# Moving the end of each projection half two dense parts further on in a stick-breaking attention stage

## The reference, cut to what matters

```python
x = x + 0.5 * swiglu(rmsnorm(x, ffn1_norm))
h = rmsnorm(x, mix_norm)
q_sb, k_sb, v_sb, q_d, k_d, v_d, q_x, gates = split(h @ w_in)
...
o_sb = stick_breaking(q_sb, k_sb, v_sb)          # 6 heads of 64
#   z = q k^T / 8; log_keep = log_sigmoid(-z) below the diagonal
#   a = exp(log_sigmoid(z) + sum of log_keep over later keys); o = a v
o_dil = dilated(q_d, k_d, v_d); o_x = memory_attention(q_x, mem)
x = x + merge(gates, o_sb, o_dil, o_x) @ w_out
x = x + 0.5 * swiglu(rmsnorm(x, ffn2_norm))
```

## Time and profile before

| | us |
|---|---|
| median of three runs (2323.61 to 2325.2) | 2324.48 |
| the profiled execution's own time | 2322.87 |
| its span, first to last instruction | 2321.1 |
| PE busy / DVE busy / ACT busy / POOL busy | 2293.4 / 1146.5 / 619.7 / 137.6 |
| PE busy in 0 to 60 us | 52.23 of 60 |
| PE busy in 785 to 1030 us (the stick-breaking stage and its rims) | 233.65 of 245 |
| PE busy in 1030 to 2321 us | 1284.11 of 1291 |

### The profile page before, as it was taken

How to read it: one execution, slowest core, us unless ns; L and a number is a source line. 1 busy time by engine, 2 the same in 40 slices (tenths; PEclk the granted TensorE clock), 3 DMA queues, 4 the chain that set the end, 5 groups by cost and what they waited for, 6 DMA issues and landing times.

```text
span 2321.1 us, 25822 instructions
## 1 busy us (share of the span) xinstructions
PE 2293.4 (99%) x10616; PEld 1855.9 (80%) x10616; DVE 1146.5 (49%) x1119; ACT 619.7 (27%) x800; POOL 137.6 (6%) x108
## 2 busy tenths in 40 slices
PE   8999999999999999999999999999999999999999
PEld 7888888888887766777778888888888888888887
DVE  8444443434445777778636333435434434444434
ACT  6211111111112567856443111224111111111111
POOL 3000000000001311222000000011000000000000
PEclk9999999999999999999999999999999999999999
DMA  5211111111112200011122111131111111111112
GB/s 163 75 46 55 45 39 52 54 45 54 45 45 70 109 28 19 19 42 41 38 28 73 46 54 55 53 120 46 46 55 45 45 54 45 50 40 54 45 54 73
DMA packets 47424, 125.78 MB, mean 54 GB/s; under 512 B 4285, under 2 KB 20829, under 8 KB 47104
## 3 DMA queue, kind: packets, MB, share of 16 engines
q1 hardware_dynamic: 45456, 112.61, 15.6%
q10 hardware_dynamic: 912, 10.11, 1.1%
q0 software_dynamic: 992, 2.15, 0.4%
HBM read 116.42 MB, written 9.87 MB: 54 GB/s over the span
## 4 chain that ended last, share of the span: by engine, by line
PE 91%; DVE 5%; ACT 2%; issue 1%; POOL 0%; DMA 0%; ACTq 0%; DVEq 0%
PE ps L1565 90%; DVE h_lo L1031 1%; PE ps L2091 0%; ACT sb_l L843 0%; DVE sp_lo L1299 0%; ACT sb_l L841 0%; DVE xT L1207 0%; DVE xT L1095 0%; PE ps L2026 0%; DVE h_lo L1491 0%; ACT sb_a L845 0%; PE ps L2183 0%; DVE w_lo L1024 0%; ACT sb_l L849 0%; DVE sb_a L1306 0%
## 5 line engine op out<-in xcount | busy, mean ns | idle before, releaser
L1565 PE MATMUL ps<-h_hi,w_hi 128*128 128x512 f32 x2240 | 872.6, 394 | 8.0 <-DVE pr_x L1324 3.6
L1565 PE MATMUL ps<-h_lo,w_hi 128*128 128x512 f32 x2240 | 862.9, 390 | 0.8 <-DVE h_lo L1491 0.6
L1565 PE MATMUL ps<-h_hi,w_lo 128*128 128x512 f32 x2240 | 700.2, 390 | 0.0
L1565 PEld LDWEIGHTS ps<-h_hi,w_hi 128*128 128x128 f32 x2240 | 420.0, 188 | 110.7 <-issue 19.2
L1565 PEld LDWEIGHTS ps<-h_hi,w_lo 128*128 128x128 f32 x2240 | 420.6, 188 | 88.7 <-DVE w_lo L1024 0.3
L1565 PEld LDWEIGHTS ps<-h_lo,w_hi 128*128 128x128 f32 x2240 | 420.6, 188 | 86.2 <-DVE h_lo L1491 1.7
L651 ACT ACTIVATE w_hi<-raw 128x1024 fp32r<-128x1024 f32 x196 | 204.3, 1052 | 794.3 <-PE ps L1565 774.1
L1024 DVE TENSOR_TENSOR w_lo<-raw,w_hi 128x1024 fp32r<-128x1024 f32 x196 | 251.3, 1290 | 157.7 <-ACT w_hi L651 149.0
L1095 DVE TENSOR_TENSOR xT<-xT,ps 128x1024 f32<-128x1024 f32 x175 | 213.4, 1219 | 173.3 <-PE ps L1565 173.1
L1565 PE MATMUL ps<-a_hi,w_hi 128*128 128x512 f32 x704 | 275.4, 391 | 1.1 <-DVE xT L1095 1.1
L1565 PE MATMUL ps<-a_lo,w_hi 128*128 128x512 f32 x704 | 274.3, 390 | 0.0
(11 more groups left out here) (234 smaller groups left out, 1579.4 us busy)
## 6 DMA issues: line engine op xcount, KB each, us to landing
raw<-in_weights SPq DMA_DIRECT2D x196, 512.0 KB, 3.5
x_keep<-xT ACTq DMA_DIRECT2D x1, 4096.0 KB, 12.7
x_back<-x_keep ACTq DMA_DIRECT2D x1, 4096.0 KB, 13.2
x_nat<-in_x SPq DMA_DIRECT2D x7, 512.0 KB, 7.5
out<-y_nat SPq DMA_DIRECT2D x7, 512.0 KB, 3.2
toe_keep<-toe_row ACTq DMA_DIRECT2D x2, 704.0 KB, 6.2
m_nat<-in_mem SPq DMA_DIRECT2D x1, 1024.0 KB, 8.0
d_fB<-d_f_keep POOLq DMA_DIRECT2D x2, 512.0 KB, 6.7
```

What stands on the lines that cost most here:

```text
L1565: return pe.matmul(o, a, b, start=start, stop=stop, skip_group_check=True)
```

## The change

Two edits. The first moves the scaling of the memory (`m_nat`, two instructions on ACT) at the start ahead of `gain_hi(6)` and `square(0, 6)`. The second moves the end of every half: k = 6 and 7 now stand in the following even step, ahead of the carry in every such step; k = 0 of the next half stands in front of that step's `sb_within`; k = 1 and 2 stand ahead of the carry in the odd step and k = 3 to 5 behind it. In step 1 it is k = 3 and 4 ahead and k = 5 behind. The copy out, `qk_hi`, `qk_lo` and `v_out` move with it on ACT and DVE.

```diff
 def half_done(s):
-    return s // 2 if s % 2 and s >= 0 else None
+    return s // 2 - 1 if s % 2 == 0 and s else None
...
+                    if k == 6:
+                        act.wait_ge(m_rs_done, 2)
+                        for b in range(MB):
+                            nc.scalar.activation(m_nat[:, b, :], m_nat[:, b, :], ACT.Copy, scale=m_rs[:, b:b + 1]).then_inc(m_scaled, 1)
                     act.wait_ge(xT_done, k + 1)
                     gain_hi(k, 0)
                 square(0, k)
...
-                if is_qk(half_done(s - 1)):
-                    qk_hi(half_done(s - 1))
+                if is_qk(half_done(s)):
+                    qk_hi(half_done(s))
...
                 if s:
                     sb_add(s - 1)
-                if is_v(half_done(s - 1)):
-                    v_out(half_done(s - 1))
-                if xq_at(s - 4) == 0:
-                    xq_scale(0)
-                if xq_at(s) is not None:
+                if half_done(s) is not None:
+                    beside_copy(half_done(s))
+
+                if xq_at(s) in (2, 3):
+                    if xq_at(s) == 2:
+                        xq_scale(0)
+                    else:
+                        v_out(half_done(s))
                     xq_keep(xq_at(s))
                 if s + 1 < SB_STEPS:
                     sb_softplus(s + 1)
+                if xq_at(s) in (0, 1):
+                    xq_keep(xq_at(s))
+                if is_v(half_done(s)) and xq_at(s) is None:
+                    v_out(half_done(s))
                 if s % 4 == 2:
                     split_lo(beside_unit(s // 4) + AHEAD)
                 if is_qk(half_done(s - 1)):
                     qk_lo(half_done(s - 1))
                 if s and chain_last(s - 1):
                     sb_out(s - 1)
-                if half_done(s) is not None:
-                    beside_copy(half_done(s))
...
                 if odd:
-                    beside(s, -1, 2)
+                    k0, k1 = (3, 5) if s == 1 else (1, 3)
+                    beside(half, k0, k1)
                     sb_carry(s - 1)
-                    beside(s, 2, 4)
-                held = is_v(half_done(s - 1)) or xq_at(s) is not None
-                if s and not odd and not held:
-                    beside(s, 0, 2)
+                    beside(half, k1, 6)
+                if s and not odd:
+                    beside(half - 1, 6, 8)
                     sb_carry(s - 1)
...
-                if held:
-                    sb_carry(s - 1)
                 if s and not odd:
                     sb_values(s - 2)
                     sb_values(s - 1)
-                    beside(s, 0 if held else 2, 3)
+                    beside(half, 0, 1)
```

More of the change, by code:

```diff
@@ L195, in beside_unit @@
     return U_SB + 3 + b
-def beside_half(s):
-    return s // 2
 def half_done(s):
-    return s // 2 if s % 2 and s >= 0 else None
+    return s // 2 - 1 if s % 2 == 0 and s else None
 def is_v(half):
@@ L785, in _ @@
                     nc.scalar.activation(m_rs[:], m_rs[:], ACT.Exp, scale=-0.5).then_inc(m_rs_done, 1)
[L786 to L789, removed]
             split_hi(2)
@@ L1387, in _ @@
                     sb_out(s - 1)
-                if half_done(s) is not None:
-                    beside_copy(half_done(s))
             sb_add(SB_STEPS - 1)
+            beside_copy(2 * BESIDE - 1)
             x_lowest(0)
@@ L1924, in sb_values, with beside @@
                 last.then_inc(sb_av, 1)
-            def beside(s, i, j):
-                half = beside_half(s)
+            def beside(half, k0, k1):
                 b, cols = half_of(half)
-                u, k0 = beside_unit(b), 4 * (s % 2) + i
+                u = beside_unit(b)
                 if k0 == 0:
@@ L1936, in beside @@
                         pe.wait_ge(bs_v, halves_before(half, is_v))
-                    if xq_at(s) is not None:
-                        pe.wait_ge(xq_kept, xq_at(s) + 1)
-                for k in range(k0, k0 + j - i):
+                    if xq_at(2 * half) is not None:
+                        pe.wait_ge(xq_kept, xq_at(2 * half) + 1)
+                for k in range(k0, k1):
                     mm(beside_bank, w_hi[:, u % NW, k, :], hh(k)[:, cols], k == 0, False)
@@ L1988, in _ @@
             for s in range(SB_STEPS):
-                odd = s % 2
+                odd, half = s % 2, s // 2
                 if odd:
-                    beside(s, -1, 2)
+                    k0, k1 = (3, 5) if s == 1 else (1, 3)
+                    beside(half, k0, k1)
                     sb_carry(s - 1)
-                    beside(s, 2, 4)
-                held = is_v(half_done(s - 1)) or xq_at(s) is not None
-                if s and not odd and not held:
-                    beside(s, 0, 2)
+                    beside(half, k1, 6)
+                if s and not odd:
+                    beside(half - 1, 6, 8)
                     sb_carry(s - 1)
@@ L2001, in _ @@
                     sb_scores(s + 3)
-                if is_v(half_done(s - 1)):
-                    v_turn(half_done(s - 1))
+                if is_v(half_done(s)):
+                    v_turn(half_done(s))
                 if xq_at(s) is not None:
                     xq_sum(xq_at(s))
-                if held:
-                    sb_carry(s - 1)
                 if s and not odd:
@@ L2014, in _ @@
                 sb_within(s)
+            beside(2 * BESIDE - 1, 6, 8)
             pe.wait_ge(xq_kept, 4)
```

## The result

| | before | changed |
|---|---|---|
| median (22 runs each) | 2324.08 | 2327.98 |
| fastest to slowest | 2322.53 to 2325.58 | 2324.62 to 2331.17 |
| the profiled execution's span | 2321.1 | 2326.3 |

The ratio is 1.0017 [1.0011, 1.0023]: 3.9 us slower, where 1.1 us faster was forecast, and 1.4 us outside the range. The changed kernel's runs are also spread over 6.6 us, those of before over 3.1.

What follows compares the result with a forecast made beforehand. PE was taken as the bound, busy 99% of the span, so only its waits could be won. The second edit's -2.3 and the first's +1.2 made -1.1 us, from 2324.48 to 2323.4; range 2320.3 to 2326.6.

Steps and rivals of the forecast that it cites:

- The waits of the stage: Second edit, stick-breaking stage: 14.9 us of PE waits replaced by 12.6 us of new ones, 2.3 won.
- full-width carries: Stage, twelve carries behind two dense parts: each 0.1 late plus 0.1 of slower restart, 2.4 us in all.
- the adds behind a weight split in steps 3, 15 and 27: Stage, adds on DVE queued behind a weight split: estimated 0.3 us each, 0.9 together.
- Halves 5 and 11: Steps 10 and 22, k = 0 waits for v_out behind the whole softplus: 2.3 us each, 4.6 together.
- the start-up: Step 2: the wait moves from k = 0 to the carry and keeps its size, 1.9 us.
- The last carry: Step 35, waiting for add(34), which comes late on DVE: 2.2 us late, 2.3 with restart.
- the other reading: Start: if only the casts shared the port lock with POOL, ones_r would end at 38.7, costing 0.1 us.
- The rival that the start wins its 0.9: No turns of POOL and DVE at the start, second edit as summed: -3.2 us, 2321.3; chance 0.10.
- a wait costs its idle plus 0.26: Unit for every PE wait in the stage: idle time plus 0.26 us for hidden lateness and slower restart.
- The slower rival: Odd steps' carry becomes the bound, the lost 0.69 exposed 18 times: about +10 + 1.2 us, 2335.7; chance 0.07.
- places only change: Stage waits only move, second edit 0, the first edit's 1.2 us loss is left: 2325.7; chance 0.25.
- all waits go: DVE has time to spare for v_out and add(34): second edit wins 9.2, total -8.0, 2316.5; chance 0.08.

Runs made afterwards that it cites:

- start_filled: Changed kernel with seven unused matmuls put on PE behind the fourth mT, ahead of norm_sum(0)'s wait; 2325.15 us, 1.0011 against before.
- w_later: Changed kernel with the weight splits of steps 10, 22 and 34 moved one step later; 2324.17 us, 1.0006 against before.
- casts_early: Changed kernel with the casts of ones_r and head_r ahead of h_lo of tile 6; 2321.86 us, 1.0001 against before.
- carry3: Changed kernel with three dense parts ahead of the odd steps' carry instead of two; 2321.91 us, 0.9998 against before.

## Why the prediction was wrong

- **The waits of the stage: the mechanism was right, the size 0.7 off.** The sum was 14.9 against 12.6, 2.3 won. Without the falls the stage won 1.6. Ten full-width carries came out as forecast (0.11 late, 0.12 slower). Two, in steps 7 and 19, showed idle at full width, one of the signs of being wrong that I had named: I had counted the adds behind a weight split in steps 3, 15 and 27 alone. They cost 0.45 each, which makes the twelve 3.1 against 2.4. Halves 5 and 11 had 2.26 idle, 2.5 in my unit instead of 2.3, twice; the wait for `xq_keep(3)`, 0.2 idle and 0.5 in my unit, was not in the sum; the start-up had 1.39 idle, 1.65 in place of 1.9. The last carry was 2.3, as forecast. The terms named here were 1.4 too small together, and the stage is off by 0.7; what makes up for the rest the runs don't show.
- **The first edit: right.** The forecast was 1.2 lost, by turns of POOL and DVE; `start_filled` measured 1.2 with the clock held. The Trainium skill, "SBUF — State Buffer", section "SBUF: two separate sides", says that the shared port pair is held for a whole instruction, by a VectorE instruction with two SBUF inputs too; the trace agrees (`h_lo` 2.65 beside POOL's adds; the cast 2.41 behind them, 0.21 ahead of them), and the other reading, by which only the casts take part (0.1 lost), is out. The rival that the start wins its 0.9 failed, because of the casts alone.
- **The step that failed:** "a wait costs its idle plus 0.26". I worked out three waits of 2.2 to 2.4 (halves 5 and 11, step 35), and a fourth of that length followed from my own numbers at the start (`norm_sum(0)` 1.2 later, PE 0.9 earlier), and ended each at its own length. The longest waits of the kernel before in these stretches are 1.7 and 1.5, with a clock of 1.00 behind them, so its rows had no price for a longer one. I had to bound it, and did not. What the runs showed in its place is the clock: three of the four waits were followed by matmuls at 1.2 GHz, for 1.40 + 1.53 + 1.56 = 4.5 us. With it and the 0.7 the sum is -1.1 + 4.5 + 0.7 = 4.1, against 3.9 measured.
- **The range** ended at 2326.6 for the same reason: the bounds were all bounds of waits. The slower rival named the wrong mechanism. The odd carries did not bind (1.7 us in all, where the rival had +10), and the others ("places only change", "all waits go") did not happen.

How often a given wait makes the clock fall is open. Nine of the kernels have such waits, 21 in their profiles, and the clock fell behind 13: behind `norm_sum(0)`'s (2.00 to 2.02) in 4 of 6, behind those of halves 5 and 11 (2.26) in 4 of 10, never behind both of one execution, and behind the last carry's (2.00 to 2.01) in 5 of 5. So the longest fell least often, and the length alone doesn't decide. What does, no run here shows. These are one execution of each kernel; the clocks of the others (0.996 to 0.998 in the changed kernel) say that the number of falls varies.

## What to carry to other kernels

In this kernel a few short waits were cheaper than one long one of the same sum: a wait of TensorE of 2.0 to 2.3 us cost, in 13 of 21 cases, more than half as much again behind it, because the clock fell. When a change gathers waits, list the longest, not only the sum, and ask whether rows of before cover that length; where they don't, price both outcomes in the range. And before an instruction is moved to start earlier, look at what its engine does later for that, and whether a small instruction elsewhere (here a cast of 128 columns) stands behind the shared port.

## What the hardware showed that I had not expected

- TensorE's granted clock went from 2.4 to 1.2 GHz behind waits of 2.0 to 2.3 us, and dense matmuls of 512 columns then started 0.42 us apart instead of 0.23. Each fall cost 1.3 to 1.6 us before the clock was back. The Trainium skill, "TensorE: Matmul & The Clock Gate", Part 1, says that the array runs at one of these two clocks by how busy it has been lately. The trace agrees: it shows 1.00 and 0.50, and the falls stand behind idle time.
- The same wait of the same length does not always do it: 2.02 in front of `norm_sum(0)` did in the changed kernel and did not in `w_later`; halves 5 and 11 wait 2.26 each, and the clock fell behind the first in one execution, behind the second in another (`start_filled`) and behind neither in a third (`casts_early`). Behind waits of 1.80 and 1.82 (`carry3`), 1.7 and 1.51 no profile shows a fall. Such waits also go with a wider spread of the times: 6.6 us with four of them, 4.1 to 5.1 with three, 1.1 to 3.1 with none.
- A cast of 128x128 that asks while POOL adds is not slowed but held until the add ends: it lasts 2.41 us, ends 0.08 behind the add (41.12 and 41.04), and lasts 0.21 where no add is under way.
